# Three pads in SBUF: the moving forms of the up product begin 32 bytes in front of a multiple of 64, the two large regions on a multiple of 64 bytes

## The reference

```python
u = rmsnorm(h, g_mix);  z = u @ w_in            # 8 HGRN2 heads, 4 GLA heads
h = h + concat(hgrn2(z), gla(z)) @ w_out        # chunkwise gated recurrences, head norms, gates
m = rmsnorm(h, g_mlp) @ w_up                    # 2048 x 8192
h = h + square(relu(m)) @ w_down                # 8192 x 2048
h = h + sigmoid(rmsnorm(h, g_ple) @ w_pg) * (p @ w_pp)
out = rmsnorm(h, g_final)
```

## The kernel before, in words

| tensor | before | mod 64 | mod 128 | after | mod 64 | mod 128 |
|---|---|---|---|---|---|---|
| `u_hi`, `forms`, `x3` (region 0) | 16512 | 0 | 0 | 16576 | 0 | 64 |
| `u_lo` | 49280 | 0 | 0 | 49408 | 0 | 0 |
| `xs`, first half (j = 2, 3) | 16512 | 0 | 0 | 16544 | 32 | 32 |
| `xs`, second half (j = 4, 5) | 49280 | 0 | 0 | 49376 | 32 | 96 |
| `w_hi`, `w_lo`, `w_raw` | 98432, 114816, 82048 | 0 | 0 | 128 more | 0 | 0 |
| `y`, `x1` (region 1), `h`, `x2`, `ring`, `raw2`, `araw`, `stage` | 135264 and on | 32 | 96 | 135424 and on | 0 | 0 |
| `xd`, `x11` | 135264, 168032 | 32 | 96 | 135392, 168160 | 32 | 96 |
| `zf`, `zq`, `zv`, `kk`, `b`, `tmp`, `kl`, `ql`, the `_back` tiles | 168032 and on | 32 | 96 | 160 more | 0 | 0 |
| `masks`, `zg`, `ez`, `norm`, `A`, `V` | 200320 and on | 0 | 0 (first) | 160 more | 32 | 32 (first) |

## Time and profile before

### The profile page before, as it was taken

How to read it: one execution, slowest core, us unless ns; L and a number is a source line. 1 busy time by engine, 2 the same in 40 slices (tenths; PEclk the granted TensorE clock), 3 DMA queues, 4 the chain that set the end, 5 groups by cost and what they waited for, 6 DMA issues and landing times.

```text
span 2427.2 us, 34799 instructions
## 1 busy us (share of the span) xinstructions
PE 2396.7 (99%) x13375; PEld 2083.6 (86%) x13375; DVE 1940.0 (80%) x2589; ACT 1203.2 (50%) x1787; POOL 50.1 (2%) x79
## 2 busy tenths in 40 slices
PE   8999999999999999999999999999999999999997
PEld 7888888888777888999999999988888888888885
DVE  6777777788887447988888888899999999995456
ACT  6444444444445235666666666643333333345345
POOL 4000000000000000000000000000000000000111
PEclk9999999999999999999999999999999999999999
DMA  6322323333224234666666666697564575633322
GB/s 176 87 77 79 86 71 84 87 85 81 78 75 149 88 131 137 183 203 201 199 198 199 197 196 196 199 354 259 197 232 161 190 257 195 229 132 115 112 86 98
DMA packets 381406, 373.71 MB, mean 154 GB/s; under 512 B 5532, under 2 KB 311352, under 8 KB 379224
## 3 DMA queue, kind: packets, MB, share of 16 engines
q1 hardware_dynamic: 381240, 371.88, 48.0%
q10 hardware_dynamic: 32, 0.01, 0.0%
HBM read 304.76 MB, written 67.11 MB: 153 GB/s over the span
## 4 chain that ended last, share of the span: by engine, by line
PE 62%; DVE 4%; ACT 1%; issue 1%; DMA 0%; DVEq 0%; ACTq 0%; SPq 0%
PE bank L2341 20%; PE bank L2343 20%; PE bank L2342 20%; DVE w_lo L2082 1%; DVE h L2128 0%; DVE w_lo L1945 0%; ACT w_hi L1161 0%; DVE w_lo L2219 0%; PE bank L2728 0%; DMA ring<-in_w_down 0%; PE bank L2623 0%; DVE gate_e L2245 0%; DVE h L2248 0%; PE bank L2419 0%; ACT gate_inv L1373 0%
## 5 line engine op out<-in xcount | busy, mean ns | idle before, releaser
L2341 PE MATMUL bank<-u_hi,w_hi 128*128 128x512 f32 x896 | 366.1, 409 | 2.7 <-DVE w_lo L1484 2.1
L2343 PE MATMUL bank<-u_hi,w_lo 128*128 128x512 f32 x896 | 350.2, 391 | 0.0
L2341 PE MATMUL bank<-w_hi,forms 128*128 128x512 f32 x896 | 349.5, 390 | 0.4 <-DVE h L2128 0.4
L2342 PE MATMUL bank<-u_lo,w_hi 128*128 128x512 f32 x896 | 349.8, 390 | 0.0
L2343 PE MATMUL bank<-w_hi,forms 128*128 128x512 f32 x896 | 348.6, 389 | 0.0
L2342 PE MATMUL bank<-w_lo,forms 128*128 128x512 f32 x896 | 348.6, 389 | 0.0
L2341 PE MATMUL bank<-xs,w_hi 128*128 128x256 f32 x1024 | 289.9, 283 | 1.3 <-DVE w_lo L1945 1.0
L2342 PE MATMUL bank<-xs,w_hi 128*128 128x256 f32 x1024 | 289.6, 283 | 0.0
L2343 PE MATMUL bank<-xs,w_lo 128*128 128x256 f32 x1024 | 289.5, 283 | 0.0
L1291 ACT ACTIVATE w_hi<-ring 128x1024 fp32r<-128x1024 f32 x124 | 132.0, 1066 | 214.8 <-PE bank L2343 140.9
L1484 DVE TENSOR_TENSOR w_lo<-w_raw,w_hi 128x2048 fp32r<-128x2048 f32 x70 | 160.1, 2287 | 63.6 <-ACT w_hi L892 63.5
(11 more groups left out here) (315 smaller groups left out, 5246.5 us busy)
## 6 DMA issues: line engine op xcount, KB each, us to landing
w_raw<-in_w_in SPq DMA_DIRECT2D x56, 1024.0 KB, 5.6
forms_scratch<-stage SPq DMA_DIRECT2D x32, 1792.0 KB, 11.2
forms<-forms_scratch SPq DMA_DIRECT2D x56, 1024.0 KB, 7.8
ring<-in_w_down SPq DMA_DIRECT2D x39, 1024.0 KB, 5.2
w_raw<-in_w_up SPq DMA_DIRECT2D x32, 1024.0 KB, 7.7
raw<-in_w_up SPq DMA_DIRECT2D x32, 1024.0 KB, 7.6
w_raw<-in_w_down SPq DMA_DIRECT2D x25, 1024.0 KB, 5.4
ring<-in_w_pg SPq DMA_DIRECT2D x18, 1024.0 KB, 5.0
```

Of the source, the lines that this page charges most:

```text
L2341: pe.matmul(ps, whi, xhi, start=start, stop=False, skip_group_check=shared)
L2342: pe.matmul(ps, whi, xlo, start=False, stop=False, skip_group_check=shared)
L2343: return pe.matmul(ps, wlo, xhi, start=False, stop=stop, skip_group_check=shared)
```

## The change

A pad of 64 bytes is allocated in front of `u_hi`, one of 64 bytes between `u_hi` and `u_lo`, and one of 32 bytes in front of `y`. `xs`, `xd` and `x11` are laid 32 bytes in front of where their regions begin; the first bytes of `xs` and `xd` fall into the pads. The two halves of `xs` are set 64 bytes further apart, since `u_lo` is. No instruction, wait, transfer or size of an operand is added, removed or moved in its order.

```diff
-        region0 = -(-nc.sbuf_base // 64) * 64
+        pad0 = sb("pad0", [P, 32 + 32 * (-(-nc.sbuf_base // 32) % 2 == 0)], U8)
+        region0 = nc.sbuf_base
+        assert region0 % 64 == 0
         u_hi = sb("u_hi", [P, KT, S], F32R)
+        pad2 = sb("pad2", [P, 64], U8)
         u_lo = sb("u_lo", [P, KT, S], F32R)
...
+        pad1 = sb("pad1", [P, 32 + 32 * (-(-nc.sbuf_base // 32) % 2 == 0)], U8)
         reg1, reg2 = ExitStack(), ExitStack()
         region1 = nc.sbuf_base
+        assert region1 % 64 == 0
         y = sb("y", [P, KT, S], stack=reg1)
...
-        xs = at("xs", region0, [P, 2, 4, 2, 2, 2, HALF], F32R)
-        xd = at("xd", region1, [P, 2, KT // 2, 2, HALF], F32R)
-        x11 = at("x11", region1 + KT * D, [P, KT // 2, 2, HALF], F32R)
+        xs = at("xs", region0 - 32, [P, 2, KT * S + 16], F32R)[:, :, 0:KT * S]\
+            .rearrange("q a (n j i l s) -> q a n j i l s", n=4, j=2, i=2, l=2)
+        xd = at("xd", region1 - 32, [P, 2, KT // 2, 2, HALF], F32R)
+        x11 = at("x11", region1 + KT * D - 32, [P, KT // 2, 2, HALF], F32R)
```

## The result

The changed kernel takes **2439.84 us** (median of five runs, 2439.37 to 2440.0). Beside it the kernel before took 2427.95 (2427.66 to 2430.27). The ratio is 1.0047, with an interval of 1.0036 to 1.0058: it is slower by 11.9 us, where 7.0 us less were forecast, and the time lies outside the range. The profiled execution spans 2438.2 us against 2427.2.

The account below looks back on a forecast made before the run. The prediction took TensorE to bound the kernel; 4.5 us in up, 2.0 in gate and 0.5 in mix made 7.0 us off the 2427.2 us span, and with 0.9 us between span and median 2421.1 us, range 2417 to 2425.

Parts of the forecast that it names:

- What bounds the kernel: Whole kernel: TensorE, busy in 99% of the span; only the speed of its matmuls can change the time.
- (a): Up: moving operand `xs` goes to 32 modulo 64, its matmuls from 120.0 to 118.3 ns; minus 4.5 us.
- (b): Gate: stationary `x1`, `x2` go to 0 modulo 64, saving 6.6 ns a matmul; minus 2.0 us.
- (c): Mix: small fp32 matmuls whose operands change place modulo 64; minus 0.5 us, at most 1.4.
- (d): Costed at nothing: large operands keeping their place modulo 64 in mix, out, down; VectorE, ScalarE and transfers.
- The pairs of the earlier trace: Same-shape matmuls compared: up's moving operand 1.5 to 1.7 ns faster off multiples of 64, gate's stationary one 6.6 slower.
- the block that straddles: Gate: a stationary operand off a multiple of 64 bytes needs one more 64-byte block read, costing 6.6 ns.
- the region rival: Up and gate: the low or high region, not the start, sets the distance; pads do nothing, 2428 us; chance 0.13.
- 6.6 ns is 16 columns: Gate: at 0.417 ns a column the stationary cost equals 16 columns, and 16 fp32 words are 64 bytes.
- unit of 128: Down, out, gate: stationary operands 64 past a multiple of 128 lose 6.6 ns each; slower, 2444.8 us; chance 0.05.
- half: Up: the saving needs 96 modulo 128, so only the second half of `xs` gains; 2423.3 us; chance 0.10.

Follow-up runs that it names:

- f1_kept: Changed kernel with spacers of 64 and 512 bytes, so stationary and moving operands stay 0 apart modulo 256 in mix, out, down; 2422.49 us.
- a_both0: Changed kernel with two pads of 128 bytes, putting `u_hi`, `u_lo` and the weights on multiples of 128; 2447.98 us.
- c1_rel224: Changed kernel re-padded: large operands 96 past multiples of 128, stationary-to-moving distance 0 modulo 256 in mix, out, down, gate, 224 in up; 2416.44 us.
- g1_reg1: Kernel before with only region 1 moved by 32 bytes, shifting `x1`, `x2`; `xs`, `xd`, `x11` stay; 2426.56 us.
- z1_pad2: Kernel before with nothing but the 64-byte pad between `u_hi` and `u_lo`; 2447.35 us.
- k1_xd80: Against the kernel before: up's weights start 64 bytes past `xs`, `x11` and 80 past `xd`, modulo 256; 0 for mix, out, down, gate; 2408.73 us.

## Why the prediction was wrong, point by point

- **What bounds the kernel: right.** TensorE's distances alone moved the time, and the difference of span, 11.0 us, is the sum of the stage table to 0.1.
- **(a) `xs`: the size right, the reason not.** Up fell by 5.3 us where 4.5 were expected. The four products read 117.8, 117.8, 118.2 and 118.3 ns, where 118.3 was said; the first two (D = 96) were somewhat better than the row from which they were priced. `f1_kept` has 4.2 us. But it was not the 32 bytes off a multiple of 64: `a_both0` keeps them for the first half of `xs` and has 120.0 ns. That the change put both halves at a D (96, 32) that is faster than 0 was luck.
- **(b) `x1`, `x2`: the size right, by luck too, then partly given back.** The z = 0 to 3 block reads 21.76 us. The gain came because the move also brought D from -32 to 0; in `c1_rel224` `x1` and `x2` lie 32 past a multiple of 64 at D = 0 and have 226.7 ns. Alone (`g1_reg1`) the part is worth 1.7 us in gate, against 2.0. In the changed kernel gate fell by only 1.0, because `x3` and the `p` tiles went from 226.7 to 228.9 ns, which the prediction had at nothing.
- **(c) the small fp32 matmuls: not there.** `g1_reg1` moves the same tiles and its mix stage is 755.5 us against 755.6. The median distance of those of L2381 is 112 ns before and after. The 0.5 us was a guess between bounds, and should have stayed in the range.
- **(d) is the step that failed.** "`u_hi`, `u_lo`, `w_hi`, `w_lo`, `forms`, `x3` keep their place modulo 64, so mix's large products, out and down stay at 226.7 ns." They kept it modulo 64 and did not stay: mix +11.6 us, down +5.6. `u_hi` moved by 64 bytes and `w_hi` by 128, and it is the 64 between them that costs, as `z1_pad2` shows without a change of place of `u_hi`. Mix lost most because its moving operands then alternate between D = 64 and 0: the 912 on `u_lo`, themselves at D = 0, grew by 7.7 us, more than the others. The rest of (d), that VectorE and ScalarE lose nothing, held: `w_lo` from `ring` 1215 ns and from `w_raw` 1219 against 1218 and 1221 in the earlier trace rows.
- **Why it failed.** The pairs of the earlier trace rows were right, but in each of them two things changed at once, the operand's own start and its distance from the weights, and the weights lay on a multiple of 64 in all rows. The prediction saw "own start modulo 64" and the block that straddles; the region rival named one confound and not the other. The working that 6.6 ns is 16 columns, hence 64 bytes, fits well and proved nothing: at D = -64 `forms` and `x3`, still on a multiple of 64, cost 2.2 ns more.
- **The rival "unit of 128"** had the place right in down and the sign of the whole, and its signal, "if down's distance grows, the unit is 128", came. But its price was three times too high (2.2 ns a matmul, not 6.6), mix was missing from its places, and its mechanism is refuted by `a_both0`, `c1_rel224` and `f1_kept`. The other rivals are out too: the region by `f1_kept`, "half" by the 117.8 and 118.3 ns of both halves.
- **What it leaves of the ports and cachelines.** The Trainium skill's page TensorE: Matmul & The Clock Gate, Part 2 (What happens when you issue a matmul), gives TensorE two independent SBUF read ports, one for the streaming and one for the weight operand. If the two reads never met, the place of one beside the other could not matter; here D alone moves a matmul of 512 columns between 226.7 and 234.1 ns. Whether they meet in SBUF or later, no run shows. The cachelines of 16 bytes in the Trainium skill (SBUF — State Buffer, Specifications (TRN2)), cited in the prediction against the change, don't explain it either: D = 16 and D = 0 are 6.7 ns apart, and so are D = 32 and D = 0.

**What stays open.** No run shows why the pattern repeats after 256 bytes, or why D = 0 is best for 512 columns and nearly worst for 256. What sets the rhythm at D = 64 is open too: the matmuls ahead take part, but how far back they count, and whether the other engines' traffic counts as well, was not tried. In `z1_pad2` there is a like case for 512 columns: `x3` and `p` at D = -64 run at 233.3 ns behind an `x1`, `x2` block of 233.3, and at 228.9 in the changed kernel, behind 226.7. Which stationary operand counts was not separated, the matmul's own or that of the next one, which is loaded while it runs (PEld is busy 49 of TensorE's 60 us in mix and down): `w_hi` and `w_lo` lie alike modulo 256 in every run. Nor is it explained what alternating D costs: 64 and 0 in mix slow both kinds of matmul, 128 and 0 (`a_both0`) only those at 128, 232.4 and 229.0 ns beside 226.8. Whether mix, out and down have a faster rhythm than 226.7 ns (which is just twice 113.3) was not tried.

## What to carry to other kernels

Before a pad goes in, write down for each large matmul the distance between its two operands modulo 256 before and after, not each start alone; a pad that moves one of them and not the other is a change to every product that they share. Two operands that differ in speed by their place are evidence for a rule only if their partners lie at different places too, so vary one by one, as a kernel with a single pad does, before adding the prices up. And where a kernel's runs scatter by more than its neighbours', look for a stream with two rhythms in the timeline: the median of such a kernel is an accident, and a neighbour of it may hold the faster one for good.

## What was not expected of the hardware

- The distance between float32r matmuls depends on D: 226.7 to 234.1 ns at 512 columns, 113.3 to 120.0 at 256, with a granted clock of 1.00 throughout and the same instructions.
- The best D found is not the same for both shapes: 0 for 512 columns, 64 for 256.
- The same matmuls on the same bytes run at 113.3 or at 117.8 ns, by what ran ahead of them, and keep it for hundreds of microseconds.
- When moving operands at two D alternate (mix after the change, 64 and 0), both pay: six in a row read 235, 239, 234, 236, 237 and 226 ns, though those at D = 0 alone would have 226.7.
- A start 16 bytes off shows nothing else: `xd` at D = 80 in `k1_xd80` costs VectorE, which writes it, no time that the page of the profile shows (1939.4 us busy against 1940.0).
